# Expert layers of a 256-token decoder trunk: routing by ranks, logits in column tiles, gate weights behind the branch, one block of column-tile products per pair

## The reference

```python
gl = einsum('btd,dg->btg', x, w_group) + b_group           # 4 group logits
pg = softmax(gl); gval, gidx = top_k(pg, 1)                # best group
il = einsum('btd,dge->btge', x, w_inner) + b_inner         # 4 x 4 expert logits
il_sel = il of the chosen group; pi = softmax(il_sel)
ival, iidx = top_k(pi, 2)                                  # two best experts in it
weight = gval * ival / sum(ival)
h = silu(x @ w_gate[e]) * (x @ w_up[e])                    # 1024 -> 256, for each expert e
y = sum over the two chosen e of (h * weight[e]) @ w_down[e]   # 256 -> 1024
```

## Time and profile before

| | us |
|---|---|
| median of 3 runs (752.06 to 759.21) | 753.58 |
| the profiled execution, its own time | 757.62 |
| span of the profiled execution | 755.8 |
| PE busy in the span | 682.8 |
| DVE busy | 367.8 |
| ACT busy | 268.6 |
| POOL busy | 91.2 |

### The profile page before, as it was taken

The page is one execution under the profiler, slowest core; times in us unless marked ns, Lnnn a source line. Parts: engine busy times, 40 slices in busy tenths (PEclk is TensorE's granted clock), DMA queues, the critical chain, the costliest instruction groups (busy, mean ns, idle before and its releaser), DMA issues.

```text
span 755.8 us, 14301 instructions
## 1 busy us (share of the span) xinstructions
PE 682.8 (90%) x6229; PEld 465.8 (62%) x6229; DVE 367.8 (49%) x611; ACT 268.6 (36%) x351; POOL 91.2 (12%) x110
## 2 busy tenths in 40 slices
PE   2799989989988798999999879999799889999984
PEld 1576757778787677444444369987577854444432
DVE  3884979533865744113222554677724521332324
ACT  3354634442533232222222263665622222222212
POOL 9810134120230100000000000022110000000000
PEclk9999999999999898999999999999989799999997
DMA  9941353000001499699999313534009979999901
GB/s 260 304 151 68 127 213 99 5 4 3 5 4 58 140 357 310 224 358 365 364 367 398 104 48 113 167 118 153 8 1 336 365 263 330 365 365 366 337 1 58
DMA packets 97732, 145.16 MB, mean 192 GB/s; under 512 B 4744, under 2 KB 70448, under 8 KB 97664
## 3 DMA queue, kind: packets, MB, share of 16 engines
q1 hardware_dynamic: 96848, 142.28, 55.5%
q0 software_dynamic: 816, 1.90, 1.1%
HBM read 143.11 MB, written 1.05 MB: 191 GB/s over the span
## 4 chain that ended last, share of the span: by engine, by line
PE 78%; DVE 12%; ACT 4%; issue 4%; DMA 1%; DVEq 0%; SPq 0%; ACTq 0%
PE ps L2245 15%; PE ps L2258 8%; PE ps L1706 7%; PE ps L1707 6%; PE ps L1708 6%; PE ps L2189 4%; PE ps L2274 4%; PE ps L1690 2%; DVE w_lo L1079 2%; PE ps L1749 2%; PE ps L2232 2%; PE ps L1861 2%; PE ps L2094 2%; PE ps L1868 1%; PE ps L1854 1%
## 5 line engine op out<-in xcount | busy, mean ns | idle before, releaser
L2245 PE MATMUL ps<-load,xe 128*64 128x512 f32 x384 | 89.5, 601 | 2.2 <-ACT xe L740 2.2
L1079 DVE TENSOR_TENSOR w_lo<-w_ring,w_hi 128x2048 fp32r<-128x2048 f32 x32 | 75.5, 2365 | 17.1 <-PE ps L1708 15.8
L665 ACT ACTIVATE w_hi<-w_ring 128x2048 fp32r<-128x2048 f32 x32 | 61.0, 1912 | 57.7 <-PE ps L1708 47.6
L1706 PE MATMUL ps<-w_hi,xa_hi 128*128 128x512 f32 x128 | 53.8, 420 | 14.8 <-DVE xa_lo L1342 8.8
L1707 PE MATMUL ps<-w_lo,xa_hi 128*128 128x512 f32 x128 | 52.5, 410 | 0.0
L1708 PE MATMUL ps<-w_hi,xa_lo 128*128 128x512 f32 x128 | 52.2, 408 | 0.0
L2245 PEld LDWEIGHTS ps<-load,xe 128*64 128x64 f32 x384 | 24.7, 136 | 42.4 <-issue 39.0
L647 POOL TENSOR_TENSOR att<-att,causal 128x256 f32<-128x256 f32 x16 | 14.9, 953 | 292.8 <-ACT att L1016 292.8
L1248 DVE TENSOR_TENSOR y_lo<-ps,y_hi 128x1024 fp32r<-128x1024 f32 x14 | 17.2, 1225 | 66.3 <-ACT y_hi L758 66.3
L747 ACT ACTIVATE silu_s<-ps 128x256 f32<-128x256 f32 x16 | 6.2, 385 | 113.9 <-issue 93.8
L2258 PE MATMUL ps<-load,hs 128*64 128x512 f32 x192 | 44.1, 601 | 0.0
(11 more groups left out here) (342 smaller groups left out, 1416.7 us busy)
## 6 DMA issues: line engine op xcount, KB each, us to landing
load<-in_moe_w_gate_dram SPq DMA_DIRECT2D x48, 512.0 KB, 8.5
load<-in_moe_w_up_dram SPq DMA_DIRECT2D x48, 512.0 KB, 8.8
load<-in_moe_w_down_dram SPq DMA_DIRECT2D x48, 512.0 KB, 8.3
w_ring<-in_rw_w_rkv_dram SPq DMA_DIRECT2D x24, 512.0 KB, 5.6
w_ring<-in_moe_w_gate_dram SPq DMA_DIRECT2D x16, 512.0 KB, 8.7
w_ring<-in_moe_w_up_dram SPq DMA_DIRECT2D x16, 512.0 KB, 9.0
w_ring<-in_moe_w_down_dram SPq DMA_DIRECT2D x16, 512.0 KB, 8.0
w_ring<-in_w_kv_dram SPq DMA_DIRECT2D x16, 512.0 KB, 5.0
```

Source lines behind the costliest of these rows:

```text
L665: nc.scalar.activation(whi[n % HI][:, :, :], w_ring[n % RING][:, :, :], ACT.Copy).then_inc(hi_ready, 1)
L1079: nc.vector.tensor_tensor(wlo[n % LO][:, :, :], w_ring[n % RING][:, :, :], whi[n % HI][:, :, :].bitcast(f32), ALU.subtract).then_inc(lo_re ...
L1706: nc.tensor.matmul(dst, xh, wh, start=start, stop=False)
L2245: m = nc.tensor.matmul(PS[rows(c), 4, :], xe[:, b, rows(c)], w[c][:, i, :], start=b == 0, stop=b == NC - 1)
```

## The change

**Router.** `wr` is padded to 32 columns. The logits are 8 products with the router weights stationary (32 columns) and 256 columns of `xT` moving, four of them in the four column strips of the array, two for each strip. ACT copies the sum to `lgT`, and two products with `add_tiles` add the strips and turn them. The expert choice compares each logit with the other three of its set at once, so that a rank (0 to 3) comes out of four instructions, and `chosen` of one more for the groups and two (`among`) for the experts. `chosen`, `ones` and `causal` are in fp32r. `place_in` counts from 1 and is 0 where a token is not chosen, so that `pick_pair` is one instruction of 256 elements. `xT` is copied bank by bank, with ACT's second row split behind its copies, and `xt_lo` goes to POOL. The gate weights and their exponentials go behind the branch (`gate_weights`, `gate_exps`), and `stay_warm(8, 5)` is dropped; a `stay_warm(5, 3)` comes in after the logits.

**First pair.** Rows and channels are copied in halves, and `turn_rows(0)` and the first `gate_up` come ahead of its gates.

**Pairs.** Both halves of `gate_up(p)` and `down(p-1)` follow each other directly; all else comes after them. `gather(p+2)` is a pair earlier and writes banks 0 and 1 (which `y_part` has to have left), and `y_hi` and `y_lo` have two buffers. At the last pair DVE and ACT do two `next_dense` each ahead of `gated` and silu, and the two row tiles of `combine` use different banks. At the program's start POOL gets 11 small instructions more ahead of its router transfers, and one among the masks.

```diff
+            def moe_phase(k):
+                s = moe_sems
+                for j in range(NT):
+                    pool.wait_ge(s["xt_hi"], k * PER["xt_hi"] + j + 1)
+                    nc.gpsimd.tensor_tensor(xt_lo[:, j, :], xs[:, j, :], xt_hi[:, j, :].bitcast(f32), ALU.subtract
+                                            ).then_inc(s["xt_lo"], 1)
...
+                row_hi(0)
+                for i in range(2):
+                    act.wait_ge(*nm.at("turned", i + 1))
+                    nc.scalar.activation(xT[:, 2 * i:2 * i + 2, :].rearrange("p b t -> p (b t)"), PS[:, 4 + i, :],
+                                         ACT.Copy).then_inc(s["xT_act"], 1)
+                row_hi(1)
+                act.wait_ge(s["lgT_psum"], k * PER["lgT_psum"] + 1)
+                nc.scalar.activation(lgT[:, :], PS[:, 0, 0:T], ACT.Copy).then_inc(s["lgT"], 1)
...
+                nc.vector.tensor_tensor(r_cmp[:, :, :, 0:EG], other, own, ALU.is_ge)
+                link(nc.vector.tensor_tensor(r_cmp[:, :, :, EG:2 * EG], other, own, ALU.is_gt))
+                flat = r_cmp[:, :, :, :].rearrange("p n i j -> p n (i j)")
+                link(nc.vector.tensor_tensor(flat, flat, rank_mask[:, :, :].rearrange("p i j -> p (i j)").unsqueeze(1)
+                                             .broadcast_to([P, NS, 2 * EG * EG]), ALU.mult))
+                link(nc.vector.tensor_reduce(rank[:, :, :].rearrange("p j (s i) -> p (j s) i", i=EG), r_cmp[:, :, :, :],
                                              AX.X, ALU.add))
-                link(nc.vector.tensor_reduce(r_s[:, 2, :], r_il[:, :, :], AX.X, ALU.max))
-                link(nc.vector.tensor_tensor(r_d[:, :, :], r_il[:, :, :], bc(r_s[:, 2, :], EG), ALU.subtract))
-                link(nc.vector.tensor_scalar(r_f1[:, :, :], r_d[:, :, :], 0.0, None, ALU.is_equal))
-                first_of(r_f1[:, :, :], r_f1[:, :, :])
-                link(nc.vector.scalar_tensor_tensor(out=r_d2[:, :, :], in0=r_f1[:, :, :], scalar=-3.0e38,
-                                                    in1=r_d[:, :, :], op0=ALU.mult, op1=ALU.add))
-                nc.vector.tensor_reduce(r_s[:, 3, :], r_d2[:, :, :], AX.X, ALU.max).then_inc(s["m2"], 1)
-                dve.wait_ge(s["m2"], k * PER["m2"] + 1)
-                link(nc.vector.tensor_tensor(r_f2[:, :, :], r_d2[:, :, :], bc(r_s[:, 3, :], EG), ALU.is_equal))
-                first_of(r_f2[:, :, :], r_f2[:, :, :])
-                link(nc.vector.tensor_tensor(r_f12[:, :, :], r_f1[:, :, :], r_f2[:, :, :], ALU.add))
-                nc.vector.tensor_tensor(chosen[:, :, :].rearrange("p j (g e) -> p j g e", g=G),
-                                        r_fg[:, :, :].unsqueeze(3).broadcast_to([P, NT, G, EG]),
-                                        r_f12[:, :, :].unsqueeze(2).broadcast_to([P, NT, G, EG]), ALU.mult
-                                        ).then_inc(s["chosen"], 1)
+                link(nc.vector.tensor_scalar(r_fg[:, :, :], rank[:, :, 0:G], 0.5, None, ALU.is_lt))
+                for j in range(NT):
+                    m = among(chosen[:, j, :], j, 1.5)
+                m.then_inc(s["chosen"], 1)
...
+                pick_pair(k, 1)
+                gate_weights(k)
                 gates_out(0)
-                pick_pair(k, 1)
                 pick_pair(k, 2)
                 for p in range(NP):
-                    if p >= 3:
-                        add_rows(p - 3, 1)
+                    if p == NP - 1:
+                        next_dense(k, 0)
+                        next_dense(k, 1)
+                    gated(p)
                     if p < NP - 1:
                         gates_out(p + 1)
-                        if p + 3 < NP:
-                            pick_pair(k, p + 3)
-                    gated(p)
+                    if p + 3 < NP:
+                        pick_pair(k, p + 3)
+                    if p:
+                        y_part(p - 1)
                     if p >= 2:
                         add_rows(p - 2, 0)
+                        add_rows(p - 2, 1, 2 if p == NP - 1 else 6)
...
-                pe.wait_ge(s["xT_act"], k * PER["xT_act"] + 1)
-                pe.wait_ge(s["xT_dve"], k * PER["xT_dve"] + 1)
+                for b in range(NC):
+                    if b % 2 == 0:
+                        pe.wait_ge(s["xT_act" if b < 4 else "xT_dve"], k * 2 + b % 4 // 2 + 1)
+                    o = slice(b % 4 * LT, (b % 4 + 1) * LT)
+                    m = nc.tensor.matmul(PS[o, 0, 0:T], wr[k][:, b, :], xT[:, b, :], start=b < 4, stop=b >= 4)
+                m.then_inc(s["lgT_psum"], 1)
+                stay_warm(5, 3)
+                pe.wait_ge(s["lgT"], k * PER["lgT"] + 1)
                 for j in range(NT):
-                    for b in range(NC):
-                        m = nc.tensor.matmul(PS[:, 0, j * NR:(j + 1) * NR], xT[:, b, j * P:(j + 1) * P],
-                                             wr[k][:, b, :], start=b == 0, stop=b == NC - 1)
+                    m = nc.tensor.matmul(PS[:, 0, j * NR:(j + 1) * NR], lgT[:, j * P:(j + 1) * P],
+                                         add_tiles[:, 0:NR], start=True, stop=True)
                 m.then_inc(s["logits"], 1)
...
-                if p:
-                    pe.wait_ge(packed_sems[k]["x_out"], p)
+                if p >= 2:
+                    pe.wait_ge(packed_sems[k]["rows_out"], 3 * p - 1)
+                if p >= 3:
+                    pe.wait_ge(packed_sems[k]["y_lo"], 2 * p - 4)
...
-                stay_warm(8, 5)
+                        combine(p, j, a, bank + a)
+
+                turn_rows(0)
                 turn_pick(0)
-                pe.wait_ge(moe_sems["gates_parts"], k * PER["gates_parts"] + 1)
-                gather_gates(0)
-                turn_rows(0)
                 for p in range(NP):
                     more = p < NP - 1
-                    if p and more:
-                        gather(k, p + 1)
-                        turn_pick(p + 1)
-                    gate_up(p, 0, (0, 1, 2, 3))
+                    gate_up(p, 0)
                     if p == 0:
                         gather(k, 1)
                         turn_pick(1)
+                        pe.wait_ge(moe_sems["gates_parts"], k * PER["gates_parts"] + 1)
+                        gather_gates(0)
+                    gate_up(p, 1)
+                    if p:
+                        down(p - 1)
                     if more:
                         gather_gates(p + 1)
-                    gate_up(p, 1, (0, 1))
+                    if p:
+                        turn(p)
                     if more:
                         turn_rows(p + 1)
-                    gate_up(p, 1, (2, 3))
+                    if p == 0:
+                        turn(p)
                     if p >= 2:
                         combine_rows(p - 2, 0)
-                    if p:
-                        down(p - 1)
-                    turn(p)
+                    if p + 2 < NP:
+                        gather(k, p + 2)
                     if p >= 2:
-                        combine_rows(p - 2, 1)
-                pe.wait_ge(s["y_lo"], 2 * (NP - 1))
-                for j in (1, 0):
-                    if j == 0:
-                        pe.wait_ge(s["added"], 4 * (NP - 2))
+                        combine_rows(p - 2, 1, 6 if more else 2)
+                    if p + 2 < NP:
+                        turn_pick(p + 2)
+                down(NP - 1)
+                for j in range(NT):
+                    pe.wait_ge(s["added"], 4 * (NP - 3) + 2 * j + 2)
                     for a in range(2):
                         combine(NP - 2, j, a, (2 if j else 6) + a, last=False)
```

292 lines of the change are left out of this document (159 added, 133 removed).

## The result

The changed kernel takes 723.88 us (median of 4 executions, 723.1 to 725.86), beside 753.58 for the kernel before (3 executions, 752.06 to 759.21): ratio 0.9592, 95% interval 0.9528 to 0.9657. Executions more than 1.5% above the fastest of their kernel count in no median or ratio here: one of before (764.17; with it the median would be 756.39), five more of before beside the experiments, and one of kernel 8 of the experiments (839.2; with it 718.86). Forecast were 720.0 and 711 to 733, so the time lies inside the range, 3.9 us above the forecast. The profiled execution took 724.1 us with a span of 721.9; worked from the profile of before, 723.2 was forecast for it.

A forecast was written before the change was run, and what follows sets the result against it. PE's own sequence was taken to bound the pairs, waits through DVE, ACT and dummy products the router stages and layer ends. Savings of 18.2 and 16.2 us took 757.6 to 723.2, 719.2 as median; forecast 720, range 711 to 733.

The forecast's parts named there:

- (a) to (f): Router stage, six parts: xT copy, logits, choice, places, pick, gather to gate_up; together 9.3 us saved in layer 0.
- its last step: Router stage: one stretch at the lower clock remains and costs 1.2 us, cutting layer 0's saving from 9.3 to 8.1.
- (b): Router logits: eight products, four strips at a time, take 0.9 us; one after another 3.4, then 0.5 lost instead.
- Gate weights: Moved behind the branch: ready about 4.5 us after gate_up starts, wanted at 5.7; if late, PE waits at most some 2.
- the sum of 16.25: Pairs 2 to 5: one run of 10.45 us plus 5.8 for the rest, 0.67 saved in each.
- PE reaches the gather at +2.75 in pairs 2 to 5: just covered: After down, y_lo is done at +2.65 us, so the gather that needs its banks does not wait.
- rival A: Pairs: new waits for y_lo take back what the new order gives, pairs stay at 16.9 us; 727 us, chance 0.15.
- Pair 1's wait: With no combine between, PE arrives at +1.8 us and waits 0.9 for y_lo; 0.55 lost in the pair.
- 10.45 + 10.8: Layer's end: last gate_up and down(6) as one run of 10.45 us, then 10.8 to the last addition.
- B: Router and layer ends: strips don't overlap, dummies bind, a second lower-clock stretch comes in each layer; 728.6 us, chance 0.12.
- C: Router choice: POOL's split falls into the rank chain, comparisons wait up to 2.5 us a layer; up to 725, chance 0.10.
- D: Weight loads: transfers become the bound if their rate falls, with about 8 us left; 764 us at 300 GB/s, chance 0.02.

The follow-up runs named there:

- kernel 8: Changed kernel with y_lo ahead of the pick on DVE and pair 4's second combine in banks 0 and 1: 717.73 us, ratio 0.9488.
- kernel 1: Changed kernel with the pairs back in their old order, new router and first pair kept: 742.15 us, ratio 0.9764.
- kernels 2 to 6: Five separate edits of the changed kernel; the first puts gate weights and exponentials ahead of the branch again: 724.93 us, ratio 0.9547. The others have their own lines.
- kernel 7: Changed kernel with the pick of a pair made by four instructions again instead of one: 726.93 us, ratio 0.9640.
- Kernel 4: Changed kernel without the four groups of dummy products in the router stage: 727.52 us, ratio 0.9595.
- kernel 3: Changed kernel with all eight logit products in one column strip, one after another: 726.75 us, ratio 0.9621.
- kernel 5: Changed kernel with fewer dummy products in both router stages, five to two behind the logits and six to three ahead of the gather: 727.26 us, ratio 0.9638.
- kernel 6: Changed kernel with POOL's second xt_lo half waiting for the logits, so it runs beside DVE's comparisons: 728.31 us, ratio 0.9648.
- kernel 10: Changed kernel with the edits of kernel 8, and dummy products trimmed in layer 1's router stage only: 715.50 us, ratio 0.9455.
- kernel 9: Changed kernel with the edits of kernel 8 and the fewer dummy products of kernel 5 in both layers: 723.15 us, ratio 0.9543.

## Why the prediction was right

**What bounds.** PE's own sequence in the pairs, and the chain around it at both ends of a layer: kernel 1 gives back one part and kernels 2 to 6 move the other, and each stays in its place.

**Router stage, (a) to (f).** Measured from the start of xs, logits begin 0.98 earlier than before (forecast 0.95), lg comes at +7.91 (forecast +7.86), the choice takes 2.40 (2.5), gather to gate_up 3.53 (3.4), and in kernel 7 the longer pick costs 0.18 (forecast 0). Without its last step the sum says 25.18 - 9.3 = 15.9, and 15.75 was measured. The step that failed is its last: "I expect one stretch at the lower clock to remain and to cost 1.2". None remained, in either layer and in all three profiles of the changed kernel, worth 2.4 of the 2.6 us. Kernel 4 shows that this is the dummy products' doing. Of the two ends in (b), kernel 3 excludes the upper one: eight products one after another cost 2.75 more.

**Gate weights.** Forecast ready 4.5 us after gate_up's start and wanted at 5.7; gates_lo ended 4.0 after it and PE read them at 5.7. The cover held, and it was ACT's table load in front of xg that the move removed.

**Pairs.** gate_up and down are one run of 10.45 as forecast (356.05 to 366.50), and kernel 8's pairs of 16.2 show that the sum of 16.25 was right for a nearly unobstructed PE (its gather still starts 0.12 behind its place and 0.14 after y_lo's end). What failed is "PE reaches the gather at +2.75 in pairs 2 to 5: just covered". y_lo came at +2.69 (forecast 2.65), but PE was there at +2.54, 0.2 before the forecast, and the gather starts at +2.83; 0.18 a pair is the price, by pair 5 and by kernel 8. That is rival A's mechanism at a quarter of its price. Pair 1's wait was 1.06 instead of 0.9. Pair 6 lost 0.45 against 0.4, and kernel 8 shows its place: the 1.06 us wait for the additions, and with other banks the pair is 1.18 shorter.

**Tail.** From the last gate_up 21.82 instead of 10.45 + 10.8 = 21.25. Of the gain of 4.8 in layer 0, 2.9 stand against kernel 1's old order at full clock; some 1.4 of the rest go with the stretch at the lower clock, which the forecast named without a price. The order of events is as forecast, with down(7) waiting for y_lo (0.17 in the row) and combine(6) as cover; each hop was some 0.1 to 0.2 longer than I gave it: down(7) started at +2.6 instead of +2.45 from the end of down(6), and the last addition ended at +11.3 instead of +10.8.

**Rivals.** A: a small part of it, above. B: strips overlap (kernel 3), dummies bind by 0.7 us a layer (kernel 5), and without lower clock. C: avoided by 0.2 us, 2.1 us a layer where it strikes (kernel 6). D: the last load of layer 1 lands 11.1 us before its first use, where I gave 8; in kernel 10, the shortest, 8.5 remain. My 8 rested on a median of 8.3 from issue to landing; before, that last load landed at 717.8, 12.7 after its issue, which by my sum leaves only 4. Transfers kept 360 to 370 GB/s, and nothing waited for them.

**From the profile to the median.** For the profiled execution 723.2 was said and 724.1 measured. For the median I took off another 4.0, as the profile of before lay above its median; that of after lies only 0.2 above its own. So 3 of the 3.9 us between 720 and 723.88 come from this last step. The gain from median to median is 29.7 us against a forecast 33.6. Executions of the kernel before spread over 752.0 to 764.9 in the study, those of the changed kernel over 720.1 to 725.9.

**What stays open.** The +2.2 us ahead of the first router stage is no work of the change as far as the runs tell. A split of weights on DVE at 103 us starts between 102.86 and 103.08 in all 14 profiles, so POOL's new instructions at the program's start cost nothing. Behind it the profiles part: the same program gives 278.55, 278.63 and 277.11, and kernel 7, which doesn't touch this part, 275.71, below before's 276.34. The lower clock explains it in part at most: 23.9 us of it in the first of the three, but in the second 10.2, as before. Why PE stands still behind layer 0 in kernels 5 and 9, and starts late there in kernel 1, is open too. The whole times of 5, 9 and 10 agree with the profiles. That the layout of the instruction stream decides, and so another number of dummy products might stop elsewhere or nowhere, is my guess and wasn't tried.

## What to carry to other kernels

When a buffer change turns a wait on one engine into a wait on another, follow the exact order of instructions on the new releaser: a 0.43 us instruction that nobody needs yet, standing ahead of the split that PE needs, cost 0.2 us a pair, and moving it behind cost nothing. Judge a stage by its own length in the trace, which here repeats to about 0.1 us, and a version by whole executions: with fewer dummy products a stage was 0.7 us shorter, and PE stopped 130 us later at a cost of 5.9 us. Before forecasting a median, ask how far the profiled execution lies from it by chance, and don't carry that distance over to the new kernel.

## What the runs showed of the hardware

- Four column strips of the array run float32 products of 256 columns side by side: 1.00 us for eight products against 3.57 in one strip.
- A DVE comparison of 160 elements took 2.40 us instead of 0.32 beside one POOL instruction of 2.35 us, which itself was not lengthened.
- PE stood still for 3.02 and 2.35 us within a run of dummy products, in the two kernels with twelve records fewer in layer 0's router stage, and was idle for 2.47 us ahead of that run in kernel 1, each time with no releaser in the profile. In kernel 9 the granted clock fell in the stop, and the other 41 records took 7.14 us instead of about 4.8; in kernel 5 it fell 1.1 us after it.
- Without such a stop the attention part of the kernels in the new order, with the same instructions, took 139.2 to 139.7 us with 3.4 us at the lower clock in it, 139.8 to 140.8 with 6.8, and 141.0 to 141.7 with 10.2: about 0.3 us for each at the lower clock.
- With dummy products in four gaps the router stages had no lower clock, without them 6.8 us each, and were 1.45 and 1.14 us longer, even though the dummy products themselves bind by 0.7.
- A table load on ACT took 1.28 us and the next instruction started 0.01 us after its end.
